# A hybrid decoder step in full float32: side input split into its own buffers, GpSimd's weight splits written out and re-timed

## The reference, cut to what matters

```python
x = x + rmsnorm(mix, prm['g_post_mix'][i])
hf = rmsnorm(x, prm['g_pre_ffn'][i])
f = jnp.square(jax.nn.relu(hf @ prm['w_ff1'][i])) @ prm['w_ff2'][i]
x = x + rmsnorm(f, prm['g_post_ffn'][i])
gate = jax.nn.sigmoid(rmsnorm(x, prm['g_ple'][i]) @ prm['w_ple_gate'][i])
x = x + (p[i] @ prm['w_ple'][i]) * gate
```

## Time and profile before

| What | Value |
|---|---|
| time, median of 3 runs | 3750.82 us (3748.04 to 3753.1) |
| profiled execution: its own time, its span | 3750.7 us, 3748.9 us |
| busy, of the span: TensorE matmul, VectorE, ScalarE, GpSimd | 3316.5, 1485.0, 906.7, 989.7 us |
| mean granted TensorE clock | 0.94 |
| slot load `w_raw`: 1092 KB, median to landing | 5.0 us |
| reload of x for the gate, `xd_late`: 4368 KB, median to landing | 14.0 us |
| issue of slot 57's load; of `xd_late` in layer 0 | 2034.5; 2025.5 |

### The profile page before, as it was taken

How to read it: one execution, slowest core, us unless ns; L and a number is a source line. 1 busy time by engine, 2 the same in 40 slices (tenths; PEclk the granted TensorE clock), 3 DMA queues, 4 the chain that set the end, 5 groups by cost and what they waited for, 6 DMA issues and landing times.

```text
span 3748.9 us, 50836 instructions
## 1 busy us (share of the span) xinstructions
PE 3316.5 (88%) x21025; PEld 3172.7 (85%) x21025; DVE 1485.0 (40%) x1852; ACT 906.7 (24%) x1876; POOL 989.7 (26%) x226
## 2 busy tenths in 40 slices
PE   4978999984478899999999799887889999999978
PEld 4977987983357799999999698876879999999968
DVE  7714013033452533333334762265154333333474
ACT  3106125061031410000001531275141000000151
POOL 3321230310002233333333333200123333333321
PEclk8989999987688999999999899999799999999989
DMA  2221210348921112222225121100111222222411
GB/s 97 103 72 49 90 66 21 118 151 257 279 70 72 48 72 92 92 92 92 92 92 182 39 78 42 53 1 31 60 66 54 78 78 78 78 78 78 156 36 60
DMA packets 84128, 323.01 MB, mean 86 GB/s; under 512 B 19033, under 2 KB 32153, under 8 KB 66073
## 3 DMA queue, kind: packets, MB, share of 16 engines
q1 hardware_dynamic: 84000, 321.18, 24.8%
HBM read 271.98 MB, written 105.23 MB: 101 GB/s over the span
## 4 chain that ended last, share of the span: by engine, by line
issue 36%; POOL 21%; PE 20%; DMA 15%; DVE 3%; ACT 3%; SPq 2%; POOLq 0%; ACTq 0%; DVEq 0%
DMA w_raw<-in_wall 12%; POOL w_lo L643 12%; PE psum L759 11%; POOL w_hi L641 9%; PE psum L784 3%; PE psum L831 2%; PE psum L856 1%; ACT pr L1287 1%; PE psum L700 1%; DMA v_sb<-in_v 1%; SPq L542 1%; PE psum L1033 1%; PE psum L1038 1%; PE psum L958 1%; PE psum L734 0%
## 5 line engine op out<-in xcount | busy, mean ns | idle before, releaser
L641 POOL TENSOR_TENSOR w_hi<-w_raw,param 128x2184 fp32r<-128x2184 f32 x111 | 427.8, 3854 | 2703.9 <-PE psum L759 2132.0
L759 PE MATMUL psum<-h_hi,w_hi 128*128 128x364 f32 x2832 | 630.7, 331 | 42.1 <-ACT xa L1245 22.8
L759 PE MATMUL psum<-h_lo,w_hi 128*128 128x364 f32 x2544 | 567.1, 331 | 8.3 <-DVE h_hi L1678 8.3
L643 POOL TENSOR_TENSOR w_lo<-w_raw,w_hi 128x2184 fp32r<-128x2184 f32 x111 | 561.7, 5060 | 8.7
L759 PEld LDWEIGHTS psum<-h_hi,w_hi 128*128 128x128 f32 x2832 | 497.6, 190 | 43.8 <-ACT xa L1245 23.1
L759 PE MATMUL psum<-h_hi,w_lo 128*128 128x364 f32 x2304 | 512.4, 331 | 0.0
L2198 DVE TENSOR_TENSOR xa<-xa,psum 128x1092 f32<-128x1092 f32 x256 | 330.4, 1291 | 339.6 <-PE psum L759 339.4
L759 PEld LDWEIGHTS psum<-h_lo,w_hi 128*128 128x128 f32 x2544 | 445.0, 190 | 9.3 <-DVE h_hi L1678 9.0
L759 PEld LDWEIGHTS psum<-h_hi,w_lo 128*128 128x128 f32 x2304 | 403.3, 190 | 0.0
L1560 ACT ACTIVATE tmp<-tmp 128x1092 f32<-128x1092 f32 x64 | 71.5, 1118 | 1261.9 <-DVE tmp L2182 1261.9
L759 PE MATMUL psum<-hid_lo,w_hi 128*128 128x364 f32 x1536 | 339.4, 329 | 0.0
(11 more groups left out here) (313 smaller groups left out, 4467.5 us busy)
## 6 DMA issues: line engine op xcount, KB each, us to landing
w_raw<-in_wall SPq DMA_DIRECT2D x111, 1092.0 KB, 5.0
kt_sb<-in_kt SPq DMA_DIRECT2D x16, 1024.0 KB, 10.9
out_ovs<-in_v SPq DMA_DIRECT2D x8, 2032.0 KB, 15.6
x_keep<-xa SPq DMA_DIRECT2D x2, 4368.0 KB, 11.8
xd_late<-x_keep SPq DMA_DIRECT2D x2, 4368.0 KB, 14.0
out_oks<-in_kt SPq DMA_DIRECT2D x8, 1008.0 KB, 8.2
out_ovs<-in_v SPq DMA_DIRECT2D x8, 1008.0 KB, 8.8
og<-o_st SPq DMA_DIRECT2D x24, 264.0 KB, 2.0
```

Source lines behind the costliest of these rows:

```text
L641: pool.tensor_tensor(w_hi[b][:, :], w_raw[:, :], param[:, C_ONE:C_ONE + 1].broadcast_to([P, SLOT]), ALU.mult).then_inc(hi_made, 1)
L643: pool.tensor_tensor(w_lo[b][:, :], w_raw[:, :], w_hi[b][:, :].bitcast(F32), ALU.subtract).then_inc(split, 1)
L759: mm = pe.matmul(UNIT[s][:, c, :], w[:, kc, cols], x[:, kc, c * CH:(c + 1) * CH], start=first, stop=last)
```

## The change

- The side input (slots 57 and 105) is split into buffers of its own, `side_hi` and `side_lo`, which lie over `tmp` and `sq2`. All slots after it move by one in the rotation of the two buffers (`buffer_of`). Its split waits for the last low part of the feed-forward's hidden pieces, no longer for a buffer of `w_hi`.
- ScalarE's squares of the feed-forward's result go to `PLE[:, 6:8]` instead of `tmp`, and VectorE adds them from there.
- GpSimd's loop over slots is written out, and its waits are on constants. The high part is a `tensor_copy` instead of a `tensor_tensor` multiplication by a broadcast 1. Three splits in each layer get a further wait: slot 26 (`W_FF + 1`) for 16 low parts of the mixed stage's residual, slot 59 (`W_GATE`) for the first mean square of the gate, slot 60 for all 24 low parts of the gate's residual.
- In the mixed stage ScalarE makes the inverse root of column part 1 at i = 8 instead of 4, just ahead of `tail_taken(2)`, and that of part 2 at i = 13 instead of 12. TensorE does the mean square of part 2 one step earlier (kc 2 instead of 3).
- In `residual`, at the first step of a column part, the add and the low part of the part before come ahead of the new factor.

```diff
--- before.py
+++ after.py
@@ -70,6 +70,12 @@
...
 LO_MIXED_C = LO_MIXED_A + 24 + 2 * FF_BLOCKS + 24 + 8 + 9
+LO_MIXED = (LO_MIXED_A, LO_MIXED_C)
+def buffer_of(slot):
+    return (slot - sum(w <= slot for w in W_PLE)) % 2
@@ -140,10 +146,11 @@
...
         s5k = sb("s5k", 3 * ST)
-        (_, tmp, rs, sq2, rst, q_st, sm, pr, pt, o_st, stat, vs_new, ks_new, sstat, og_in, c_w, ca_e, t_e, xt3, t_tab, h0, st_o, sx,
+        (_, tmp, rs, sq2, rst, side_lo, _, side_hi, q_st, sm, pr, pt, o_st, stat, vs_new, ks_new, sstat, og_in, c_w, ca_e, t_e, xt3, t_tab, h0, st_o, sx,
...
             [("tmp", 2 * T, F32), ("rs", T, F32), ("sq2", 2 * T, F32), ("rst", 9, F32)],
+            [("side_lo", 2 * T, F32R), ("e0", T, F32), ("side_hi", 2 * T, F32R)],
@@ -632,23 +639,30 @@
...
         def _(pool):
-            raw, hi, done = Count(raw_in), Count(hi_made), Count(slot_done)
-            def split_slot(b, wait_free=True):
-                pool.wait_ge(raw_in, raw.add(16))
-                if wait_free:
-                    pool.wait_ge(slot_done, done.add())
-                pool.tensor_tensor(w_hi[b][:, :], w_raw[:, :], param[:, C_ONE:C_ONE + 1].broadcast_to([P, SLOT]), ALU.mult).then_inc(hi_made, 1)
-                pool.wait_ge(hi_made, hi.add())
-                pool.tensor_tensor(w_lo[b][:, :], w_raw[:, :], w_hi[b][:, :].bitcast(F32), ALU.subtract).then_inc(split, 1)
-            pool.wait_ge(const_in, 64)
-            split_slot(0, wait_free=False)
-            split_slot(1, wait_free=False)
-            with turns(pool, (N_SLOTS - 3) // 2, {raw: 32, hi: 2, done: 2}):
-                split_slot(0)
-                split_slot(1)
-            split_slot(0)
+            def split_slot(slot, high, low):
+                pool.wait_ge(raw_in, 16 * (slot + 1))
+                pool.tensor_copy(high[:, :], w_raw[:, :]).then_inc(hi_made, 1)
+                pool.wait_ge(hi_made, slot + 1)
+                pool.tensor_tensor(low[:, :], w_raw[:, :], high[:, :].bitcast(F32), ALU.subtract).then_inc(split, 1)
+            for slot in range(N_SLOTS):
+                if slot in W_PLE:
+                    pool.wait_ge(lo_made, LO_MIXED[W_PLE.index(slot)] + 24 + 2 * FF_BLOCKS)
+                    split_slot(slot, side_hi, side_lo)
+                    continue
+                if slot >= 2:
+                    earlier = slot - 2 - any(slot - 2 <= w < slot for w in W_PLE)
+                    pool.wait_ge(slot_done, earlier + 1)
+                for layer in range(2):
+                    if slot == W_FF[layer] + 1:
+                        pool.wait_ge(lo_made, LO_MIXED[layer] + 16)
+                    elif slot == W_GATE[layer]:
+                        pool.wait_ge(whole_sum, (5, 14)[layer])
+                    elif slot == W_GATE[layer] + 1:
+                        pool.wait_ge(lo_made, LO_MIXED[layer] + 24 + 2 * FF_BLOCKS + 24)
+                split_slot(slot, w_hi[buffer_of(slot)], w_lo[buffer_of(slot)])
@@ -673,7 +687,7 @@
...
             def halves(slot, kcs):
-                return [t[slot % 2][:, 0:2048].rearrange("p (k c) -> p k c", k=kcs) for t in (w_hi, w_lo)]
+                return [t[buffer_of(slot)][:, 0:2048].rearrange("p (k c) -> p k c", k=kcs) for t in (w_hi, w_lo)]
@@ -738,7 +752,7 @@
...
                                 mm.then_inc(slot_done if m else full, 1)
-                        if tail and c == 0 and kc == 3:
+                        if tail and c == 0 and kc == 2:
@@ -1174,8 +1188,7 @@
...
                 slot_ready()
-                s = W_PLE[layer] % 2
-                PH, PL = (t[s][:, :].rearrange("p (k c) -> p k c", k=2) for t in (w_hi, w_lo))
+                PH, PL = tiles(side_hi, 2), tiles(side_lo, 2)
@@ -1222,10 +1235,10 @@
...
-            def part(kc, half):
+            def part(kc, half, squares=TMP):
...
                 late(part_added, parts.add() - 2)
-                act.activation(TMP[:, half, :], XA[:, kc, :], ACT.Square)\
+                act.activation(squares[:, half, :], XA[:, kc, :], ACT.Square)\
@@ -1533,11 +1546,10 @@
...
                 for i in range(24):
-                    if i == 4:
+                    if i == KC:
                         inverse_of_parts(1)
-                    elif i == KC:
                         tail_taken(2)
-                    elif i == 12:
+                    elif i == 13:
@@ -1572,7 +1584,7 @@
...
                     act.wait_ge(free[kc % 2], u.free[kc % 2].at - 3 + kc // 2)
-                    part(kc, kc % 2)
+                    part(kc, kc % 2, PLE[:, 6:8, :])
@@ -1642,10 +1654,10 @@
...
-            def add_part(half):
+            def add_part(half, squares=TMP):
...
                 dve.wait_ge(part_made, pm.add())
-                dve.tensor_tensor(rs[:, :], rs[:, :], TMP[:, half, :], ALU.add).then_inc(part_added, 1)
+                dve.tensor_tensor(rs[:, :], rs[:, :], squares[:, half, :], ALU.add).then_inc(part_added, 1)
@@ -1682,31 +1694,49 @@
...
                 dve.wait_ge(x_in, xin.add(16))
-                for i in range(24 + 2):
-                    if i < 24:
-                        c, kc = divmod(i, KC)
-                        cols = slice(c * CH, c * CH + CH)
-                        if kc == 0:
-                            inverse()
-                        if tail and kc == 6:
-                            if c < 2:
-                                dve.wait_ge(tail_out, touts.add())
-                            else:
-                                dve.wait_ge(free[0], u.free[0].at)
-                                dve.wait_ge(free[1], u.free[1].at)
-                        dve.scalar_tensor_tensor(XA[:, kc, cols], XA[:, kc, cols], G[:, layer, kind, kc:kc + 1], rs[:, cols],
-                                                 ALU.mult, ALU.mult).then_inc(dve_own, 1)
-                        own.add()
+                def cut(i):
+                    c, kc = divmod(i, KC)
+                    return c, kc, slice(c * CH, c * CH + CH)
+                def scale(i):
+                    c, kc, cols = cut(i)
+                    if kc == 0:
+                        inverse()
+                    if tail and kc == 6:
+                        if c < 2:
+                            dve.wait_ge(tail_out, touts.add())
+                        else:
+                            dve.wait_ge(free[0], u.free[0].at)
+                            dve.wait_ge(free[1], u.free[1].at)
+                    dve.scalar_tensor_tensor(XA[:, kc, cols], XA[:, kc, cols], G[:, layer, kind, kc:kc + 1], rs[:, cols],
+                                             ALU.mult, ALU.mult).then_inc(dve_own, 1)
+                    own.add()
+                def add_old(i, scaled_since):
+                    c, kc, cols = cut(i)
+                    dve.wait_ge(dve_own, own.at - scaled_since)
+                    dve.tensor_tensor(XA[:, kc, cols], XA[:, kc, cols], X[:, kc, cols], ALU.add).then_inc(x_made, 1)
+                    xmd.add()
+                def low_of(i, added_since):
+                    c, kc, cols = cut(i)
+                    dve.wait_ge(x_made, xmd.at - added_since)
+                    low_scaled(low_, layer, kind + 1, kc, cols, high_)
+                for i in range(26):
+                    between_pieces = i % KC == 0
+                    if i < 24 and not between_pieces:
+                        scale(i)
                     if 1 <= i <= 24:
-                        c, kc = divmod(i - 1, KC)
-                        cols = slice(c * CH, c * CH + CH)
-                        dve.wait_ge(dve_own, own.at - (1 if i < 24 else 0))
-                        dve.tensor_tensor(XA[:, kc, cols], XA[:, kc, cols], X[:, kc, cols], ALU.add).then_inc(x_made, 1)
-                        xmd.add()
+                        add_old(i - 1, not between_pieces)
                     if i >= 2:
-                        c, kc = divmod(i - 2, KC)
-                        dve.wait_ge(x_made, xmd.at - (1 if i <= 24 else 0))
-                        low_scaled(low_, layer, kind + 1, kc, slice(c * CH, c * CH + CH), high_)
+                        low_of(i - 2, i <= 24)
+                    if i < 24 and between_pieces:
+                        scale(i)
@@ -2200,9 +2230,9 @@
...
                         if add_parts and m:
-                            add_part((m - 1) % 2)
+                            add_part((m - 1) % 2, PLE[:, 6:8, :])
                     if add_parts:
-                        add_part(1)
+                        add_part(1, PLE[:, 6:8, :])
...
                 evict(1)
```

## The result

The changed kernel takes 3696.6 us (median of 4 runs, 3688.7 to 3701.4) where the kernel before takes 3749.4: a ratio of 0.9852, with an interval from 0.9840 to 0.9865, so 51 to 60 us less. The forecast of 3695 and its range held. Several of its terms did not, and two errors stood against each other: the sections behind this one are about them.

What follows compares the result with a forecast made beforehand. GpSimd's splits were judged far from the bound; TensorE's waits at code the change touches were the target. Gains 34.4 + 2.0 + 13.8 + 3.4 + 1.7 = 55.3 us took 3750.7 to 3695, range 3686 to 3709.

Steps and rivals of the forecast that it cites:

- case 2: Rival, chance 0.20: GpSimd's one-input copy is no cheaper than the multiplication; 3695 + 5.1 + 5.8 = 3706 us.
- First wait: Before the projection: TensorE's 9.8 us wait for slot 58's split goes, and 1.9 of low clock; 11.7 per layer.
- Price of the earlier place: Slot 56: slot 58's earlier subtraction delays VectorE's adds of squares, so TensorE waits 0.9 us for a unit.
- Second wait: Before the gate: 7.65 of TensorE's 9.8 us wait for slot 59's split regained; its third-unit wait grows by 1.2.
- W_GATE + 1 held back: Gate: holding this split for 24 low parts costs nothing; split near 2137, TensorE needs it near 2148.
- Mixed tail: Before the mixed arrival: held split and new order let TensorE start at 1274.2, not 1281.10; 6.9 us per layer.
- TensorE doesn't wait there now, so 0: Mixed tail's last third: the moved mean square and third inverse root start VectorE earlier, gaining 0.
- The copy, 2.1 us: GpSimd's high part: the one-input copy takes 2.1 us against the multiplication's 3.83, so 1.7 less a split.
- It pays only where VectorE waits for GpSimd and TensorE for VectorE: The copy's gain: 3.4 us at the start and 1.7 at layer 0's end, together 5.1.
- case 3: Rival, chance 0.12: held split delays TensorE in the mixed tail, or its stall moves into slot 56; 3702 to 3709.
- Case 4: Rival, chance 0.04: at the gate TensorE waits as long for ScalarE's inverse roots and squares; 3732 us.
- case 5: Rival, chance 0.04: slower, the fp32r copy is a slow software path; at 16 us a copy, 3900 us.

Runs made afterwards that it cites:

- after_again: The changed kernel itself, unaltered, measured in a second series: 3691.6 us, 0.9838 of the kernel before.
- copy_undone: The changed kernel with the high parts made by the multiplication again instead of the one-input copy: 3723.0 us, 0.9926 of the kernel before.
- side_first: The changed kernel with SyncE issuing the loads of slots 57 and 58 before the 4.4 MB load of the old x: 3685.5 us, 0.9825.
- no_gate_holds: The changed kernel without the further waits of the two gate slots' splits (59 and 60 in layer 0): 3705.3 us, 0.9866, range 3692.4 to 3715.0.
- old_order: The changed kernel with the old order on VectorE, ScalarE and TensorE; side buffers, copy and holds kept: 3699.5 us, 0.9865.
- copy_only: The kernel before with only GpSimd's loop written out and the one-input copy; two buffers, no holds: 3729.5 us, 0.9944.
- side_only: The changed kernel with only the side buffers and moved squares left; multiplication, old orders, no holds: 3750.0 us, 0.9993 of the kernel before.

## Why the prediction was right, and where it was not

**The total.** Spans without 21-22 fell by 60.0 us (after_again); the prediction's terms gave 55.3. The attention stretch was 3.5 and 3.8 us longer in the two traces of the changed kernel, which is within its scatter; in the medians the gain is 53 and 59. That the total came so near is partly luck. By its own case 2 the prediction put everything but the copy at 44.4 us (3750.7 to 3706.3) and the copy at 10.9. copy_undone gives 36.0 for everything but the copy (3374.4 to 3338.4) and 24.0 for the copy: one term too high by 8, the other too low by 13.

**First wait, 11.7 per layer.** Right. TensorE goes from slot 56 into the projection without a pause (2073.16), mean_square follows 6.0 us later, at 2079.15, as forecast, and the clock behind it is 1.00 where it was 0.50. That 2079.15 is also near the 2079.3 on the clock of the trace before is chance: slot 55's split starts at 1997.0 where it started at 2001.6, and slot 56 then took as much longer.

**Price of the earlier place, 0.9 for a unit.** Mis-sized. Counted from the start of slot 55's split (2001.6 before, 1997.0 after), I had slot 57's split at 38.4 and slot 58's subtraction at 52.9, 2.2 us ahead of the first add of squares at 55.1 (2056.69). The loads came later than that: slot 57's split began at 40.8 and slot 58's subtraction at 55.1, 0.06 us ahead of the add, which it held for its whole length. The wait was 2.74 us in layer 0 and 2.65 in layer 1, with a low clock behind it in layer 0, and slot 56 took 4.5 us more there instead of 0.9. In after_again layer 1 paid 0.90, because there the add came first by 0.05 us and kept its length, and the subtraction and the second add (4.21 us) paid for it:

```profile
3513.85 1.29 DVE L1660 TENSOR_TENSOR rs<-rs,ple 128x1092 f32<-128x1092 f32 x1
```

```profile
3513.90 6.00 POOL L647 TENSOR_TENSOR w_lo<-w_raw,w_hi 128x2184 fp32r<-128x2184 f32 x1
```

```profile
3522.44 0.77 PE L773 MATMUL psum<-hid_hi,w_hi 128*128 128x364 f32 x3 [0.90 <-DVE xa L2228]
```

So the size hangs on a tenth of a microsecond. In side_first, where only the loads' order differs, the subtraction is at 51.7, the add still at 55.1, and the wait is gone in both layers.

**Second wait.** The gate's idle is 3.5 us, not the 2.15 that 7.65 of 9.8 left over, but little of that is lost: TensorE came earlier. Behind its waits for units it does the rest of the projection in 9.5 us (2095.67 to 2105.2) where it took 10.8 (2106.80 to 2117.6) at a clock that was low for part of it, and ScalarE's squares, which it then waits for, came 11.1 us earlier:

```profile
2108.07 2.47 ACT L1543 ACTIVATE tmp<-xa 128x364 f32<-128x364 f32 x6
```

TensorE's wait for the third unit is 2.89, against 2.17 + 1.2 = 3.4, and VectorE's first two factors took 3.66 us, about as forecast. From the end of slot 56 to the gate's first matmul the time fell by 18.65 us (54.2 to 35.55) where the prediction's 11.7 - 1.2 + 7.6 make 18.1. What is missing lies on either side: the 4.5 in slot 56, and the 1.0 for the clock, which did not come; from the gate's first matmul to slot 62's split it takes 0.9 more than before. Together I had 18.2 per layer; 55-62 gave 13.3, 103-110 gave 16.4 and, in after_again, 18.3.

**W_GATE + 1 held back: nothing is paid.** Right, no wait for w_lo is left. In the profiled execution of no_gate_holds the two holds are worth 8 and 12 us; two of its five executions were as short as the changed kernel's, so what they are worth on average stays open.

**Mixed tail, 6.9 per layer.** The size of the wait was right (6.68 left, 6.6 forecast), and the stretch lost 8.9 in all: the other 2 are the clock behind the next wait, 1.28 us for three matmuls before, 0.76 now. The reason was half of it: the prediction has the hold and the order free the piece together, and either does it alone (6.02 with the hold, 6.69 with the order). "TensorE doesn't wait there now, so 0", for the mean square and the third inverse root moved, was too low: without these moves and the new order in `residual` the held split reaches TensorE, and the stretch is 5.3 us longer (old_order).

**The copy, 2.1 us.** Right as a duration: 2.06 on average, and 2.01 where VectorE is idle. The Trainium skill (GPSIMD Engine Reference, section "When to use GPSIMD") calls such operations roughly line-rate, from which I had an estimate of 1.9; the trace agrees within about 0.1 us. **"It pays only where VectorE waits for GpSimd and TensorE for VectorE", 5.1** was the step that failed: the runs show 20 to 24. I had 3.4 at the start (in copy_only 3.4 for TensorE's first matmul, 3.9 for the stretch) and 1.7 at layer 0's end (3.5 in copy_only, with a wait of 2.40 us gone); absent from my list were SyncE's queue behind slot 6 (2 to 3), the gate (2 to 7 a layer) and the mixed tail (2 to 3 a layer). Case 2's time of 3706 would therefore have been 3723, outside the range.

**Rivals.** Of case 3 the last sentence, the same stall moved into slot 56, did happen, and under the condition named there: slot 57's load is issued behind the 4.4 MB load and its split came 2.4 us later than reckoned. It cost 1.8 us of waiting more than priced, not 7. The held split in TensorE's way shows in old_order and, smaller, in copy_undone, not in the changed kernel. Case 4 did not happen. Of case 5, a slow copy, there is no trace. What the prediction did not price at all is what the buffers are worth without the holds and the order: nothing (side_only). It gave the gate 34.4 us and did not say that they hang on the holds. The Trainium skill (SBUF — State Buffer, section on the two sides of SBUF) has the rule that when a VectorE instruction with two SBUF inputs meets a GpSimd instruction that reads SBUF, the one that starts first keeps the shared ports for its whole length. The traces agree: 5.11 and 6.00 us for VectorE operations of 0.59 and 1.29, 6.00 instead of 4.9 for a subtraction that started 0.05 us behind an add, and single operations back to their own lengths once the split is elsewhere.

## What to carry over

When a split, a cast or any long GpSimd instruction shares SBUF with a chain on VectorE, a second buffer alone may only turn one wait into another of the same length; release the long instruction by a semaphore of the chain that it would stop, at the moment when that chain waits for a third engine. Look in such a kernel for every VectorE operation that is several times as long as its twins: here those left over were worth 15 us at two places that the change had not touched. And price a shorter instruction along each in-order queue that waits for it, SyncE's DMA queue included, not only along the engines' chain.

## What was not expected of the hardware

- The granted clock fell to 0.85 and then 0.64 in the 20 us from 371 in one execution of the changed kernel and stayed at 1.00 in the other, with TensorE busy for 8.85 and 9.15 of 10 us in both. And behind two waits of the same length (3.42 and 3.43 us) it was full in one kernel and low in the other. What decides it stays open.
- Cutting a GpSimd instruction into four lets VectorE in between the pieces, at the price of both: 9.34 us for a subtraction that took 5.71 uncut in the same place, 2.43 instead of 1.29 for the VectorE operation.
- Layer 0's attention stretch took from 371.3 to 388.1 us in fourteen traces, with code that differs there in the split of one slot at most. TensorE's waits for cache loads differ from trace to trace; the cause stays open.
